# Row steps packed into the last input panels, and value products spread over four column groups

## What is computed

```python
z = x @ w_in                       # 1024 -> 2316 columns, split among four head groups
A: GLU -> causal depthwise conv (31) -> LayerNorm -> swish -> pointwise
B: 4 query heads, one K/V head: compressed blocks + selected blocks (64 rows, top 16) + window (512),
   o = g0 * o_cmp + g1 * o_sel + g2 * o_win
C: MoBA, 4 heads: the 3 best past blocks of 256 keys by q . mean(k), and the own block
D: trailing means over 2, 4, 8, 16 rows
x = LN(alpha * x + concat(A, B, C, D) @ w_out)
x = LN(alpha * x + relu(x @ w_up)**2 @ w_down)
```

## Time and profile before

| | |
|---|---|
| time, median of 3 runs | 884.84 us (884.17 to 888.94) |
| time of the profiled execution | 885.0 us |
| its span | 883.2 us |
| mean granted TensorE clock | 0.956 |
| PE busy | 795.7 us, 90%, 6793 instructions |
| DVE busy | 457.6 us, 52% |
| ACT busy | 289.4 us, 33% |
| POOL busy | 146.9 us, 17% |
| moved by transfers | 113.20 MB, mean 128 GB/s |

### The profile page before, as it was taken

How to read it: one execution, slowest core, us unless ns; L and a number is a source line. 1 busy time by engine, 2 the same in 40 slices (tenths; PEclk the granted TensorE clock), 3 DMA queues, 4 the chain that set the end, 5 groups by cost and what they waited for, 6 DMA issues and landing times.

```text
span 883.2 us, 17247 instructions
## 1 busy us (share of the span) xinstructions
PE 795.7 (90%) x6793; PEld 684.7 (78%) x6793; DVE 457.6 (52%) x832; ACT 289.4 (33%) x569; POOL 146.9 (17%) x148
## 2 busy tenths in 40 slices
PE   6999989978767798896989899999999999999983
PEld 6988877755323355552889899999999999999982
DVE  4289955465635443343476855553355335533445
ACT  4322244444454112123243445431243113411123
POOL 0003570000000000000045575100011001100073
PEclk9999999999878699998999999999999999999997
DMA  8546653536725687640123332333223332233202
GB/s 322 158 133 156 182 167 119 193 129 206 241 67 177 195 261 217 186 162 25 48 72 121 118 91 78 96 97 96 78 91 106 89 93 80 89 113 83 91 4 96
DMA packets 73291, 113.20 MB, mean 128 GB/s; under 512 B 25177, under 2 KB 42202, under 8 KB 72538
## 3 DMA queue, kind: packets, MB, share of 16 engines
q1 hardware_dynamic: 63994, 109.99, 40.2%
q10 hardware_dynamic: 9216, 2.10, 1.1%
HBM read 107.63 MB, written 6.52 MB: 129 GB/s over the span
## 4 chain that ended last, share of the span: by engine, by line
PE 70%; DVE 15%; issue 7%; ACT 4%; ACTq 2%; DMA 1%; POOL 1%; SPq 0%; DVEq 0%; POOLq 0%
PE psum L653 50%; DVE yc L1459 4%; PE psum L731 2%; PE psum L967 2%; PE psum L763 2%; PE psum L662 2%; PE psum L706 2%; PE psum L913 2%; PE psum L902 1%; PE psum L734 1%; DVE nmR L1484 1%; DVE wL L1397 1%; ACTq L1127 1%; ACT psum L1137 1%; PE psum L950 1%
## 5 line engine op out<-in xcount | busy, mean ns | idle before, releaser
L1397 DVE TENSOR_TENSOR wL<-raw,wH 128x1024 fp32r<-128x1024 f32 x90 | 118.3, 1314 | 112.7 <-ACT wH L1057 112.7
L1057 ACT ACTIVATE wH<-raw 128x1024 fp32r<-128x1024 f32 x90 | 93.7, 1042 | 128.5 <-PE psum L653 124.8
L653 PE MATMUL psum<-oxH,wH 128*128 128x260 f32 (+1 forms) x512 | 105.6, 288 | 3.8 <-DVE wL L1397 3.7
L653 PE MATMUL psum<-opH,wH 128*128 128x260 f32 (+1 forms) x416 | 89.1, 296 | 21.1 <-DVE opL L1393 8.1
L653 PE MATMUL psum<-hidH,wH 128*128 128x260 f32 x512 | 103.9, 284 | 2.6 <-issue 2.6
L653 PE MATMUL psum<-oxH,wL 128*128 128x260 f32 (+1 forms) x512 | 104.4, 285 | 0.0
L653 PE MATMUL psum<-oxL,wH 128*128 128x260 f32 (+1 forms) x512 | 104.0, 284 | 0.0
L653 PE MATMUL psum<-hidL,wH 128*128 128x260 f32 x512 | 103.7, 284 | 0.0
L653 PE MATMUL psum<-hidH,wL 128*128 128x260 f32 x512 | 103.7, 284 | 0.0
L653 PEld LDWEIGHTS psum<-opH,wH 128*128 128x128 f32 (+1 forms) x416 | 65.4, 192 | 29.6 <-issue 12.4
L653 PE MATMUL psum<-opH,wL 128*128 128x260 f32 (+1 forms) x416 | 85.5, 288 | 0.0
(11 more groups left out here) (343 smaller groups left out, 1136.7 us busy)
## 6 DMA issues: line engine op xcount, KB each, us to landing
raw<-in_panels SPq DMA_DIRECT2D x89, 512.0 KB, 3.6
moba_lo<-in_moba_pages SPq DMA_DIRECT2D x64, 256.0 KB, 3.5
moba_hi<-in_moba_pages SPq DMA_DIRECT2D x64, 256.0 KB, 3.6
nsa_ring<-in_nsa_pages SPq DMA_DIRECT2D x128, 96.0 KB, 2.2
xres<-in_xT SPq DMA_DIRECT2D x8, 260.0 KB, 6.3
xres<-in_xT SPq DMA_DIRECT2D x1, 2080.0 KB, 8.8
out_y<-xres SPq DMA_DIRECT2D x8, 260.0 KB, 2.1
selV<-in_selv_pages SPq DMA_DIRECT2D x64, 32.0 KB, 2.7
```

The source lines that it names most:

```text
L653: last = mm(out[0:M, hf, 0:cols], w, x[:, k, hf * HALF:hf * HALF + cols], start=(t == 0 and j == 0), stop=(t == KT - 1 and j == 2))
L1057: fn(wH[:, n % NW].rearrange("p a b -> p (a b)")[:, 0:m], raw[:, n % NRAW, 0:m], ACT.Copy).then_inc(h_done, 1)
L1397: tt(wL[:, n % NW].rearrange("p a b -> p (a b)")[:, 0:m], raw[:, n % NRAW, 0:m], wH[:, n % NW].rearrange("p a b -> p (a b)")[:, 0:m].bitca ...
```

## The change

It does five things.

1. ATT_PANEL is 14 and ROW_PIECES (4, 8, 8, 8): all 28 rows lie inside panels 14 to 17, 12 units instead of 10 go with them, and each panel's `evac` stands ahead of its last row. In panel 14 the last sample's `kv` and `csc` stand behind the first half of the products, `zcols` behind the second, and the four rows follow the evacuation.
2. The due times behind the panels are new: first columns at 5 instead of 8, `fina` at 9 behind the units' end instead of 2, the split of panel 19 at 20 behind it, ahead of the last `msplit`s (before, it came with panel 18). DVE work on pick and shift becomes a step `prep`; three small operations on the gates move up to `zcols`.
3. The value products of a sample go to four column groups in turn, and each sample has its own 64 columns of bank 3. `fina` sums the groups: a copy of 128 x 512 and ten small products in place of two additions and two transposes. The compressed part is scaled in `backa`.
4. One group of four 128 x 128 transposes serves all eight chunks of a sample, in place of two groups of four.
5. The pages of samples 1, 3, 5 and 7 are issued by POOL, with a wait for the units' products, and those of the other samples by SP; ACT issues none.

```diff
-ATT_PANEL = 15
-ROW_PIECES = (7, 7, 6)
-MU1, UNIT = 10, 4.4
+ATT_PANEL = 14
+ROW_PIECES = (4, 8, 8, 8)
+MU1, UNIT = 12, 4.4
...
-        if i + 1 < N_PANELS and i + 1 != OUT0:
+        if i + 1 < N_PANELS and i + 1 not in (OUT0, OUT0 + 1):
...
-        out += spread([s for q in range(n) for s in (("mm", i, q, n), ("row", first + q))], extras)
-        return out + [("evac", i)]
+        atoms = [s for q in range(n) for s in (("mm", i, q, n), ("row", first + q))]
+        if i == ATT_PANEL:
+            rows_ = [s for s in atoms if s[0] == "row"]
+            mms = [s for s in atoms if s[0] == "mm"]
+            return out + mms[:2] + [("kv", B), ("csc", 0)] + mms[2:] + [("zcols", 0), ("evac", i)] + spread(rows_, extras)
+        return out + spread(atoms[:-1] + [("evac", i), atoms[-1]], extras)
...
-    extras = {15: [("ctr", 0), ("zrow", 0), ("win", 0), ("cimp", 0), ("mu", 0)] + M(1, 2),
-              16: M(2, 4) + [("zrow", 1)] + M(4, 6),
-              17: M(6, MU1)}
+    extras = {14: [("ctr", 0), ("zrow", 0), ("win", 0)],
+              15: [("cimp", 0), ("mu", 0)] + M(1, 4),
+              16: M(4, 6) + [("zrow", 1)] + M(6, 8),
+              17: M(8, MU1)}
...
-        if i == 14:
-            tl += [("csc", 0), ("zcols", 0)]
-    head = [(0, ("out_z", 0)), (0.1, ("zrow", 2)), (0.2, ("own", 0)), (1.5, ("vrow", 0)), (2.5, ("vrow", 1)), (3, ("msplit", 0)), (3, ("msplit", 1))]
-    rows = [(0.5 + 0.8 * n, ("row", NR0 + n)) for n in range(NR - NR0)]
-    rows += [(0.3, ("lse", 0)), (5.5, ("lset", 0)), (7, ("lse", 1)), (13, ("lset", 1))]
+    rows = []
+    head = [(0, ("out_z", 0)), (0, ("prep", 0)), (0.3, ("zrow", 2)), (0.4, ("lse", 0)), (0.4, ("lse", 1)), (0.5, ("vrow", 0)), (0.6, ("vrow", 1)),
+            (2.5, ("lset", 0)), (2.6, ("lset", 1)), (2.7, ("own", 0)), (4, ("msplit", 0)), (4, ("msplit", 1))]
...
-        units += [(at_, ("mu", u)), (at_ + UNIT / 2, ("mp", u - 1))]
+        units += [(at_, ("mu", u)), (at_ + 0.5 * UNIT, ("mp", u - 1))]
...
-    join = [(9 + 2 * k, ("stat", k)) for k in range(5)] + [(18.5, ("comba", 0)), (20, ("comba", 1)), (29, ("backa", 0))]
+    join = [(8 + 2 * k, ("stat", k)) for k in range(5)] + [(17.2, ("comba", 0)), (21.2, ("comba", 1)), (26, ("backa", 0))]
     for b in range(B):
-        at_ = 33 + (end - 40) / B * b
-        join += [(at_ - 3, ("psc", b))] + [(at_ + 1.7 * c, ("st", b, c)) for c in range(3)] + [(at_ + 6, ("spv", b))]
+        at_ = 29 + (end - 38) / B * b
+        join += [(at_ - 3, ("psc", b))] + [(at_ + 1.7 * c, ("st", b, c)) for c in range(2)] + [(at_ + 6, ("spv", b))]
         if b < NRAW:
             join.append((at_ + 6, ("load_panel", OUT0 + b)))
-    join += [(end, ("msplit", 2)), (end, ("msplit", 3)), (end + 1, ("load_x", 1)), (end + 1, ("split", OUT0)), (end + 2, ("fina", 0)),
-             (end + 6, ("msplit", 4)), (end + 6, ("msplit", 5))]
+    join += [(end, ("msplit", 2)), (end, ("msplit", 3)), (end + 1, ("load_x", 1)), (end + 1, ("split", OUT0)), (end + 20, ("split", OUT0 + 1)), (end + 9, ("fina", 0)),
+             (end + 13, ("msplit", 4)), (end + 13, ("msplit", 5))]
...
-        at_ = 8 + (end - 10) / NCN * n if n < NCN else end + 1 + 2.5 * (n - NCN)
+        at_ = 5 + (end - 8) / NCN * n if n < NCN else end + 1 + 2.5 * (n - NCN)
...
-    last = [(end, ("statm", 0)), (end + 0.1, ("combm", 0)), (end + 0.2, ("combm", 1)), (end + 12, ("backm", 0)), (end + 15.5, ("mpv", 0)), (end + 19, ("finm", 0)),
+    last = [(end, ("statm", 0)), (end + 0.1, ("combm", 0)), (end + 7, ("combm", 1)), (end + 12, ("backm", 0)), (end + 15.5, ("mpv", 0)), (end + 19, ("finm", 0)),
             (end + 25, ("msplit", 6)), (end + 25, ("msplit", 7))]
...
-                elif kind == "selv" and n % 2 == 0:
+                elif kind == "selv" and n // 4 % 2 == 0:
...
-                    if c < 2:
-                        for p in range(4):
-                            q = 4 * c + p
-                            last = nc.tensor.transpose(psum[0:HD, 2, p * P:(p + 1) * P], Psel[:, n, q * HD:(q + 1) * HD], ident)
+                    if c == 0:
+                        for q in range(4):
+                            last = nc.tensor.transpose(psum[:, 2, q * P:(q + 1) * P], Psel[:, n, q * P:(q + 1) * P], ident)
...
-                        mm(psum[:, 3, 0:P], zeros[:, :], ident, start=True, stop=False, skip_group_check=True)
+                        mm(psum[:, 3, :], zeros[:, :], Psel[:, 0, :], start=True, stop=False, skip_group_check=True)
                     pe.wait_ge(selv_in[b], 16 * PAGES)
-                    c, j = b // 4, b % 4
-                    out = psum[32 * j:32 * j + H, 3, c * HD:(c + 1) * HD]
+                    out = [psum[32 * j:32 * j + H, 3, b * HD:(b + 1) * HD] for j in range(4)]
                     V = selV[b]
-                    for k in range(3):
+                    for k in range(2):
                         bank_read(pe, 2, ("st", b, k))
                     for p in range(PAGES):
-                        mm(out, PTs[:, b % 2, p // 8, p % 8, :], V[:, p, :], start=False, stop=False, skip_group_check=True)
+                        mm(out[p % 4], PTs[:, b % 2, p // 8, p % 8, :], V[:, p, :], start=False, stop=False, skip_group_check=True)
                     for w in range(4):
-                        mm(out, PTw[:, b % 2, w, :], winV[:, b, w, :], start=False, stop=False, skip_group_check=True)
-
-                    mm(out, wnew[:, 0, b, :], zs[:, 2, 0:HD], start=False, stop=False, skip_group_check=True)
-                    mm(out, wnew[:, 2, b, :], zs[:, 2, HD:P], start=False, stop=(b == B - 1), skip_group_check=True).then_inc(spv_mm, 1)
+                        mm(out[w], PTw[:, b % 2, w, :], winV[:, b, w, :], start=False, stop=False, skip_group_check=True)
+
+                    mm(out[0], wnew[:, 0, b, :], zs[:, 2, 0:HD], start=False, stop=False, skip_group_check=True)
+                    mm(out[1], wnew[:, 2, b, :], zs[:, 2, HD:P], start=False, stop=(b == B - 1), skip_group_check=True).then_inc(spv_mm, 1)
...
-                    for c in range(2):
-                        last = nc.tensor.transpose(psum[0:HD, 2, c * P:(c + 1) * P], On[:, c, :], ident)
+                    own_rows = ident.rearrange("p (j x) -> p j x", j=4)[:, :, 0:H]
+                    for b in range(B):
+                        if b % 4 == 0:
+                            mm(psum[0:HD, 2, H * b:H * b + 16], oc[:, b // 4, :], own_rows, start=True, stop=False, skip_group_check=True)
+                        last = mm(psum[0:HD, 2, H * b:H * b + H], On[:, b, :], cst[:, C_HM:C_HM + H], start=False, stop=True, skip_group_check=True)
...
-                elif kind == "selv" and n % 2 == 1:
-
-                    if n == 1:
-                        act.wait_ge(ids_in, 16)
-                        act.wait_ge(mm_done, N_IN_PANELS)
-                    for p in range(n * 4, n * 4 + 4):
-                        v = act.value_load(page_ids[0:1, p:p + 1])
-                        act.dma_start(selV[p // PAGES][:, p % PAGES, :],
-                                      a["selv_pages"][bass.ds(v, 1)].rearrange("a p n -> (a p) n")).then_inc(selv_in[p // PAGES], 16)
...
+                if kind == "selv" and n // 4 % 2 == 1:
+
+                    if n == 4:
+                        pool.wait_ge(ids_in, 16)
+                        pool.wait_ge(mm_done, N_IN_PANELS)
+                    pool.wait_ge(mp_mm, MU1 + n // 2 - 2)
+                    for p in range(n * 4, n * 4 + 4):
+                        v = pool.value_load(page_ids[0:1, p:p + 1])
+                        pool.dma_start(selV[p // PAGES][:, p % PAGES, :],
+                                       a["selv_pages"][bass.ds(v, 1)].rearrange("a p n -> (a p) n")).then_inc(selv_in[p // PAGES], 16)
...
+                    chain(ts(gT[:, :, :], gT[:, :, :], 0.5, 0.5, ALU.mult, ALU.add))
+                    chain(ts(gT[:, :, :], gT[:, :, :], 1e-30, None, ALU.max))
+                    nc.vector.reciprocal(gT[:, :, :], gT[:, :, :]).then_inc(gate_done, 1)
...
+                elif kind == "prep":
+                    dve.wait_ge(mm_done, N_IN_PANELS)
+                    nc.vector.tensor_copy(pick[:, :], cst[:, C_PICK:C_PICK + 16])
+                    ts(shift[:, :, :].rearrange("p a b -> p (a b)"), spread(cst[:, C_PICK], 2 * T), 0.0, None, ALU.mult).then_inc(pick_done, 1)
...
+                    bank_read(dve, 1, ("cimp", 0))
                     nc.vector.memset(zeros[:, :], 0.0)
+                    for c in range(2):
+                        ts(oc[:, c, :], oc[:, c, :], g0[:, c:c + 1], None, ALU.mult)
...
+                    for e in range(2):
+                        s = psum[HD * e:HD * e + HD, 2, :].rearrange("p (s j x) -> p s j x", s=4, j=4)
+                        for half in range(2):
+                            last = nc.vector.tensor_copy(
+                                PTs[HD * half:HD * half + HD, n % 2, :, e:8:2, :].rearrange("p g s h -> p s g h"),
+                                s[:, :, 2 * half:2 * half + 2, 0:H])
```

(43 more changed lines are left out.)

1 line of the change is left out of this document (removed).

## The result

The changed kernel takes 843.7 us (842.88 to 844.9, four runs) against 884.82 of the kernel before beside it: ratio 0.9527, 95% interval 0.9496 to 0.9558. The forecast was 841 in a range of 826 to 864. The profiled execution has a span of 841.6 us, 41.6 under the one before, and a granted clock of 0.965.

What follows compares the result with a forecast made beforehand. TensorE (PE), busy 90% of the span, was taken to bound C, and a chain among PE, DVE and ACT to bound B. 10.6 - 21.3 - 25.9 - 7 = -43.6 from 885.0 gave 841 us, range 826 to 864.

Steps and rivals of the forecast that it cites:

- A: Panels 14 to 17 (75.6 us): takes up 8 MoBA rows and two more units, +10.6 us (bounds 4 and 18).
- B: Last panel to first column step: a chain of single answers remains, 32.3 to 11 us, -21.3 (bounds -24 and -15).
- C: MoBA units, columns and samples' value products (128.5 us): less PE work, -25.9 us (bounds -12 and -33).
- SP gets whole samples ... units are loaded four ahead (20 us), so nothing: In C: SP's 12 transfers take 8.4 us against a 5 us unit, 3.4 late twice, hidden by early loading: no cost.
- transposes: In C: eight groups of four go, at 0.56 us, with eight handovers to the DVE: -6 us.
- ACT's pages: In C: page loads leave ACT, where four cost 2.79 us in front of the exponentials: -5 us.
- given back: In C: units follow every 5 us, and waits for own and PTm that PE work covered come out: +4 us.
- POOL: Page issue in B and C: about 1.2 us a page, hidden up to 1.45; as slower rival, chance 0.08.
- D: Last unit to first output panel (30.6 us): fina later, wait for On goes, -7 us (bounds -9 and 0).
- Loads serialise: Rival on value products: each weight load costs 93 ns, 868 us, or 859 if products merely don't overlap; chance 0.05.
- Freed time comes back as waits: Rival: unit passing or DMA engines set C; C -14, A +16, 858 us; chance 0.17.
- Signs: What the changed profile would show: spv 0.7 us a sample, On wait under 1 us, C near 103, wrong if A above 93.

Runs made afterwards that it cites:

- even pages: Changed kernel with each sample's pages shared half and half by SP and POOL, in place of whole samples in turn: 844.33 us (0.9514).
- memsets early: Changed kernel with SP issuing only samples 0 and 4, POOL the other six, and two DVE memsets moved from comba to behind stat 0: 838.79 us (0.9468).
- one column group: Changed kernel with all products of a sample's selected values in one column group again, the rest kept: 854.03 us (0.9629).
- POOL three of four: Changed kernel with SP issuing the pages of samples 0 and 4 alone and POOL those of the other six: 843.17 us (0.9518).
- schedule alone: Changed kernel's order of steps, but one column group, two groups of transposes and odd page steps on ACT as before: 865.28 us (0.9762).

## Why the prediction was right, and which terms were not

Against the forecast the four stretches are off by -0.8, -1.8, +5.2 and +1.2 us; A and B take back half of what C missed.

- **A**, +10.6: measured +9.8. From 190 us on the PE is busy for 51.9 of 53.4 us and the wait for zT is gone (taken back: right). The loss lies where it was put, at rows 0 to 3: 23 us with the PE busy for 19.5 at a clock of 0.70. That the sum fits is in part luck. The PE was busy for 16.0 us more, not 11.6: no term had the low clock, which here is some 6 us (an estimate, 0.30 of the 19.5). Its idle time fell by 6.2 us (11.8 to 5.6), not by 1.

```profile
167.00:190.00 23.00, 19.45 (x207) 13.79 (x207) 11.88 (x35) 10.90 (x47) 0.00 (x0) 0.70 0.40 152
190.00:243.40 53.40, 51.93 (x516) 31.05 (x514) 35.39 (x74) 30.25 (x113) 0.00 (x0) 1.00 0.60 196
```

- **B**, -21.3: measured -23.1. The first half of the chain is the forecast one. In its order of time:

```profile
242.61 1.24 DVE nmR L1491
...
243.87 1.45 ACT psum L1132 x4
...
245.79 1.28 ACT L1137
...
247.82 0.59 ACT Vn L1123
...
248.45 1.08 PE psum L905 x16
...
249.94 1.72 PE psum L829 x8
...
251.68 0.60 ACT shift L1143
```

 Behind Vn the PE holds it, with a unit's scores (L905, and L912 for 0.41) and the transposes into shift (L829), 3.2 us; the forecast had ACT there, with the second Vn, a table load and an exponential, 2.4 us. The DVE's part of shift takes 0.06 us on it, not 0.68. (The forecast's own pieces add up to 10.8, not 10.6; 11 was used.)
- **C**, -25.9: measured -20.7. The sizes on the PE were nearly right: L968 and L970 take 7.8 us instead of the 23.6 of before, 15.8 less (forecast 17.5 with the longer zero product counted); the transposes' busy time falls by 4.7 (forecast 4.5, and 1.5 for handovers). The step that failed is "SP gets whole samples ... units are loaded four ahead (20 us), so nothing". Its price was right (12 transfers 8.4 us; three groups at 2.40 are 7.2), its slack was not. The load of unit 24 has leave (SP may start it) when the product of unit 20 is done, and unit 24 is wanted at 316.4. On the PE and in SP's queue:

```profile
302.24 0.64 PE L916 MATMUL psum<-moba_lo,PTm 128*32 128x256 f32 x8
...
318.10 0.64 PE L905 MATMUL psum<-moba_lo,QM 128*32 128x128 f32 x16 [1.72 <-DMA moba_lo<-in_moba_pages]
```

```profile
303.80 0.85 SPq L512 DMA_DIRECT2D moba_hi<-in_moba_pages  x2
305.15 4.26 SPq L583 DMA_DIRECT2D selV<-in_selv_pages  x8
309.51 0.38 SPq L502 DMA_DIRECT2D raw<-in_panels  x1
310.41 5.03 SPq L512 DMA_DIRECT2D moba_lo<-in_moba_pages  x8
```

 From leave (302.9) to need (316.4) are 13.5 us, not 20, at unit 28 even 9.9 (product of unit 24 at 326.05, need at 336.5), because "four ahead" counts from a product that comes one and a half units late. The load itself takes some 2 to issue and 4 to land. So the slack was 4 to 7.5 us, and the rest of a unit, eight pages and a panel stood ahead for 7.5. For unit 28 that explains the wait of 2.6 us; for unit 24 it would be just in time, and the 1.7 us are that issuing took 2.6 us and its last page over 5 to land, with the DMA engines' share at 1.01 (315 to 320 us).

 Nor can SP catch up: 20 units pass in 106.0 us, 21.2 for four, and their 32 transfers are 19.2. Before, four units took 25.3 (20 in 126.7). SP's total did not change, the PE's pace did, and so did SP's order: eight pages a unit in two units of four, where it was four in each. By the run with even pages, over half of the wait (5.6 or 4.3 us down to 1.6) is the bursts'. The terms that were added up for transposes (6, found 1 to 3) and ACT's pages (5, found 1 to 3) were oversized too, and the +4 "given back" is too small.
- **POOL**: 1.2 us a page was forecast, 0.90 measured, the instruction itself 0.54. In order of time:

```profile
255.88 0.54 POOL L1330 DMA_DIRECT2D selV<-in_selv_pages  x1 [0.35 <-issue]
256.78 0.54 POOL L1330 DMA_DIRECT2D selV<-in_selv_pages  x1 [0.36 <-issue]
```

 It does not wait for landing (3.2 us). Doubling the pages showed that POOL's issue can become the bound, and the time then rose by 15 us; the break-even of 1.45 us a page for 64 pages was not tested by any run.
- **D**, -7: measured -5.8, the wait for On 1.1 us. fina's place alone is 4 to 5 us of it.
- **Loads serialise**: refuted. One column group costs the PE 56 ns an instruction, four cost 14 to 16, each with its own weights and the same row groups. By the rule of the Trainium skill, TensorE: Matmul & The Clock Gate, "Part 3: Packing small matmuls", these loads would not overlap; the trace does not agree.
- **Freed time comes back as waits** (858): true in kind, and in C under half of its size (5 of 12 us): waits for loads and PTm replaced those for own and PTw, and C is 5 us longer than forecast.
- **Signs**: no wait for selV, pages under 1.45 us apart, units 5.3 us apart, A under 93: all as stated. Just missed: the wait for On is 1.1 us and not under 1, C is 107.8 and not near 103, and the sample's product takes 0.95 us, not 0.70.

## What to carry to other kernels

When the bound engine gets faster, work out anew, for every queue, its load against the new pace and the time from leave to need of each load in it: the same queue was harmless at 19 of 25 us, issued evenly, and set part of the stretch at 19 of 21, issued in bursts. Savings found one by one under such a queue need not add up: removed singly they were worth 8, 1 to 3 and 1 to 3 us, together 20 (each figure is good to some 3 us). A setup instruction that depends on nothing late, such as a memset, is to be looked for in front of the longest wait first.

## What was not expected

The same 231 PE instructions of D took 26.6, 28.2 and 30.8 us in different kernels. The changed kernel, memsets early, one column group:

```profile
358.60:385.20 26.60, 24.22 (x231) 11.97 (x231) 13.71 (x61) 9.61 (x20) 0.00 (x0) 1.00 0.07 21
```

```profile
354.70:382.90 28.20, 25.82 (x231) 12.41 (x231) 13.72 (x61) 9.63 (x20) 0.00 (x0) 0.94 0.07 20
```

```profile
366.20:397.00 30.80, 28.80 (x231) 13.97 (x231) 13.71 (x61) 9.80 (x20) 0.00 (x0) 0.83 0.07 18
```

The DVE's and ACT's busy times are the same to 0.2 us; the granted clock alone makes 4 us. In "POOL three of four" it fell to 0.50 for 370 to 375 us behind 5 us in which the PE was busy for 3.89, a dip that the changed kernel has not. The stretch ahead of panel 14, which no edit touches, varied in the same way: panel 14 starts at 157.3 us in "schedule alone" and at 163.2 in even. A change of 2 us is therefore not to be had from one trace, nor from a sum of stages.

With all pages on POOL, its issues stand 0.90 us apart except for a few single ones (1.1 to 1.2) and three from 248.3 to 252.6 us, 1.3 to 1.6 apart, in stretch B. The DMA engines' share was 1.03 there, and the DVE was busy for 1.8 of the 4.6 us. No run here tells why.
